# Expert passes on four column tiles, activations turned in 32x32 blocks by VectorE

## The reference

```python
g = jnp.minimum(xb @ w_gate[e] + b_gate[e], SWIGLU_LIMIT)
u = jnp.clip(xb @ w_up[e] + b_up[e], -SWIGLU_LIMIT, SWIGLU_LIMIT)
act = g * jax.nn.sigmoid(SWIGLU_ALPHA * g) * (u + 1)
return act @ w_down[e] + b_down[e]
...
ys = lax.map(expert_block, (xs, block_e)).reshape(n_blocks * EXPERT_BLOCK, D)
y_pairs = ys[dest] * pair_gate[:, None]
return jnp.zeros_like(h).at[pair_tok].add(y_pairs)
```

## Time and profile before

| | |
|---|---|
| median of 3 runs | 1791.53 us (1791.15 to 1792.47) |
| the profiled execution | 1791.65 us, of which the span of instructions 1789.8 us |
| TensorE matmul (PE) busy | 1760.1 us, 98% of the span |
| TensorE weight loads (PEld) busy | 888.5 us, 50% |
| VectorE (DVE), ScalarE (ACT) busy | 39%, 21% |
| L1504, the expansions, 2112 records | 466.1 us busy |
| L1566, the down product, the 1036 records that read the ring | 229.5 us busy |
| L1515 combine, L1472 gather, L1485 biases | 67.6, 62.2 and 37.0 us busy |
| expert weights | 2 MB a load, median 25 to 28 us from issue to landing |
| mean granted TensorE clock | 0.998 of full speed |

### The profile page before, as it was taken

How to read it: one execution, slowest core, us unless ns; L and a number is a source line. 1 busy time by engine, 2 the same in 40 slices (tenths; PEclk the granted TensorE clock), 3 DMA queues, 4 the chain that set the end, 5 groups by cost and what they waited for, 6 DMA issues and landing times. The chain is left out here.

```text
span 1789.8 us, 21732 instructions
## 1 busy us (share of the span) xinstructions
PE 1760.1 (98%) x8267; PEld 888.5 (50%) x8268; DVE 689.4 (39%) x1369; ACT 368.0 (21%) x740; POOL 62.7 (4%) x55
## 2 busy tenths in 40 slices
PE   8999999999999999999999999999999999999998
PEld 6855533333333333333333334798445579864454
DVE  1774411111111111111111112666667757747765
ACT  2222311111111111111111113333221022222201
POOL 0000000000000000000000000450000000000000
PEclk9999999999999999999999999999999999999999
DMA  9967799999999999999999999733466653126462
GB/s 376 374 256 312 314 409 428 430 431 431 431 431 432 431 432 430 432 431 431 432 431 431 432 431 399 216 141 141 143 224 193 219 188 142 48 94 235 148 203 96
DMA packets 106570, 565.10 MB, mean 316 GB/s; under 512 B 19624, under 2 KB 42893, under 8 KB 80781
## 3 DMA queue, kind: packets, MB, share of 16 engines
q1 hardware_dynamic: 105588, 562.93, 78.1%
q10 hardware_dynamic: 922, 1.36, 0.3%
HBM read 553.78 MB, written 2.10 MB: 311 GB/s over the span
## 5 line engine op out<-in xcount | busy, mean ns | idle before, releaser
L1504 PE MATMUL ps<-ring,xs 128*64 128x512 f32 x2112 | 466.1, 593 | 6.2 <-DMA ring<-in_w_up 3.7
L1504 PEld LDWEIGHTS ps<-ring,xs 128*64 128x64 f32 x2112 | 150.9, 137 | 310.3 <-issue 294.0
L1566 PE MATMUL ps<-ring,actT 128*64 128x512 f32 x1036 | 229.5, 595 | 0.0
L1640 DVE TENSOR_SCALAR hT<-ps 128x512 f32<-128x512 f32 x33 | 22.8, 691 | 445.2 <-PE ps L1504 445.2
L2548 PE MATMUL ps<-ring 128*128 128x512 f32 x448 | 193.1, 593 | 1.1 <-DVE early_consts L2935 1.1
L2548 PEld LDWEIGHTS ps<-ring 128*128 128x128 f32 x448 | 108.6, 243 | 84.9 <-issue 61.0
L1566 PEld LDWEIGHTS ps<-ring,actT 128*64 128x64 f32 x1036 | 71.6, 137 | 155.6 <-issue 129.6
L1642 DVE TENSOR_SCALAR hT<-ps 128x512 f32<-128x512 f32 x33 | 22.8, 691 | 265.0 <-PE ps L1504 265.0
L2523 PE MATMUL ps<-ring,hT 128*128 128x512 f32 x192 | 84.8, 593 | 0.0
L2905 DVE TENSOR_TENSOR ring<-ring 128x2048 f32<-128x2048 f32 x32 | 72.6, 2286 | 13.5 <-PE ps L2523 7.7
L1617 ACT COPY y<-ps 128x512 f32<-128x512 f32 x33 | 19.3, 585 | 246.5 <-PE ps L1566 246.5
(11 more groups left out here) (523 smaller groups left out, 1987.6 us busy)
## 6 DMA issues: line engine op xcount, KB each, us to landing
ring<-in_w_gate SPq DMA_DIRECT2D x64, 2048.0 KB, 26.9
ring<-in_w_up SPq DMA_DIRECT2D x64, 2048.0 KB, 25.1
ring<-in_w_down SPq DMA_DIRECT2D x62, 2048.0 KB, 27.7
ring<-in_mlp_w SPq DMA_DIRECT2D x16, 2048.0 KB, 8.6
ring<-in_mlp_w SPq DMA_DIRECT2D x32, 1024.0 KB, 5.6
ring<-in_w_mod SPq DMA_DIRECT2D x8, 2048.0 KB, 12.9
ring<-in_odd_w_in SPq DMA_DIRECT2D x6, 2048.0 KB, 10.6
ring<-in_w_mod SPq DMA_DIRECT2D x16, 512.0 KB, 10.9
```

Source lines behind the costliest of these rows:

```text
L1504: mm = pe.matmul(ps[SLOTS * half:SLOTS * (half + 1), bank, :], xs[:, c % 4, c // 4 * SLOTS:(c // 4 + 1) * SLOTS], weights(v, 8 * part + c) ...
L1566: mm = pe.matmul(ps[SLOTS * half:SLOTS * (half + 1), Y, :], actT[:, f % 4, f // 4 * SLOTS:(f // 4 + 1) * SLOTS], moving, start=(f == 0), s ...
L1640: v.tensor_scalar(g, ps[:, G, :], LIMIT, None, ALU.min).then_inc(g_ok, 1)
```

## The change

The 64 slots of a pass become two groups of 32 (`TILE`), and the array is used as four column tiles of 32 instead of two of 64. Column tile j holds, for both groups, the 128 columns from 128 j of each half of the 1024 columns: group 0 lies in columns 0 to 255 of the bank, group 1 in columns 256 to 511 (`tile_columns`, `group_columns`). So an expansion has, for each block of weight rows, eight matmuls of 256 columns in place of two of 512, and the down product four matmuls of 512 columns in place of two. The biases become eight matmuls of 512 columns, each reading its 256 bias columns twice (`twice`), and a new matmul of one column goes ahead of them.

With this layout the activations can be turned inside 32x32 blocks. VectorE does it with two block transposes straight from `g` into `actT` (`turn_tiles`), which gets the shape 128 x 8 x 64. TensorE's four transposes of the activations, ScalarE's copy of them and the semaphore between them go. TensorE no longer waits for `act_ok` and `xs_sb` there, but for `u_ok`. The gathered tokens are turned by TensorE as before, and the gather and `combine` keep their shapes. SyncE's last load of the stage waits for `selt_ps` in place of `xt_ps`.

```diff
--- before.py
+++ after.py
@@ -28,7 +28,7 @@
 IN_W = FOUR + QLAT + KVLAT + ROPE
 EPS = 1e-6
 EXPERTS, TOPK, FF = 32, 4, 1024
-SLOTS = 64
+SLOTS, TILE = 64, 32
 SPARE = (SEQ * TOPK) // (SLOTS + 1)
 PASSES = EXPERTS + SPARE + 1
 LIMIT, ALPHA = 7.0, 1.702
@@ -1366,6 +1366,27 @@
     return w[0, bass.ds(e, 1), k * 512:(k + 1) * 512, :].rearrange("e (p a) n -> p (e a) n", p=P)
 
 
+def twice(a):
+
+    return a.rearrange("p (g k) n -> p g k n", g=1).to_broadcast([a.shape[0], 2, a.shape[1], a.shape[2]])
+
+
+def tile_columns(a, j):
+
+    return a.rearrange("p (k j n) -> p k j n", k=2, j=4)[:, :, j, :]
+
+
+def group_columns(a, g):
+
+    return a[:, SEQ * g:SEQ * (g + 1)].rearrange("p (k n) -> p k n", k=2)
+
+
+def turn_tiles(v, out, src, g):
+
+    blocks = src[:, SEQ * g:SEQ * (g + 1)].rearrange("p (k r a) -> p k a r", k=2, a=4)
+    return v.transpose(out[:, :, TILE * g:TILE * (g + 1)].rearrange("p (k a) n -> p k a n", k=2), blocks)
+
+
 def stage_experts(nc, m, t):
 
 
@@ -1379,14 +1400,14 @@
     xrow = s.sb("xrow", [P, 512])
     xs = s.sb("xs", [P, 4, P])
     g, u, sig = (m.hT[:, 2 * j:2 * j + 2, :].rearrange("p c n -> p (c n)") for j in range(3))
-    actT = s.sb("actT", [P, 4, P])
+    actT = s.sb("actT", [P, C, SLOTS])
     y = s.sb("y", [P, 512])
     m.even_in = [m.lasting(f"even_in{k}") for k in range(4)]
 
 
     G, U, Y, TURN, COMB = 0, 1, 2, 3, 4
-    w_free, xt_ps, down_ps, selt_ps, comb_ps, actT_ps, bias_ps, total_ps = (
-        m.sem(f"e_{n}") for n in ("w_free", "xt_ps", "down_ps", "selt_ps", "comb_ps", "actT_ps", "bias_ps", "total_ps"))
+    w_free, xt_ps, down_ps, selt_ps, comb_ps, bias_ps, total_ps = (
+        m.sem(f"e_{n}") for n in ("w_free", "xt_ps", "down_ps", "selt_ps", "comb_ps", "bias_ps", "total_ps"))
     x_ps = m.gather_ps
     sel_ok, selg_ok, now_ok, g_ok, u_ok, act_mul, act_ok = (
         m.sem(f"e_{n}") for n in ("sel_ok", "selg_ok", "now_ok", "g_ok", "u_ok", "act_mul", "act_ok"))
@@ -1459,7 +1480,7 @@
             sp.dma_start(columns(12)[:, :, 384:512], src[:, :, KWN:KWN + P]).then_inc(m.even_in[0], 16)
             sp.dma_start(columns(16), src[:, :, NQ:NQ + 512]).then_inc(m.even_in[1], 16)
             sp.dma_start(columns(20), src[:, :, MQ:MQ + 512]).then_inc(m.even_in[2], 16)
-            sp.wait_ge(xt_ps, n + 1)
+            sp.wait_ge(selt_ps, n)
             sp.dma_start(columns(0), src[:, :, MK:MK + 512]).then_inc(m.even_in[3], 16)
 
         @block.tensor
@@ -1479,12 +1500,12 @@
                 mm.then_inc(xt_ps, 1)
 
             def biases(parts):
-                for half in range(2):
+                for j in range(4):
                     for part, bank in parts:
                         a = EXPERTS * part
-                        mm = pe.matmul(ps[SLOTS * half:SLOTS * (half + 1), bank, :], now[a:a + EXPERTS, :],
-                                       m.brows[a:a + EXPERTS, half * 512:(half + 1) * 512], start=True, stop=False,
-                                       skip_group_check=True)
+                        row = tile_columns(m.brows[a:a + EXPERTS, :], j)
+                        mm = pe.matmul(ps[TILE * j:TILE * (j + 1), bank, :], now[a:a + EXPERTS, 0:TILE],
+                                       twice(row), start=True, stop=False, skip_group_check=True)
                 mm.then_inc(bias_ps, 1)
 
             def arrived(v, turn, k):
@@ -1500,10 +1521,11 @@
                 for c in range(C):
                     if c % 4 == 0:
                         arrived(v, turn, 2 * part + c // 4)
-                    for half in range(2):
-                        mm = pe.matmul(ps[SLOTS * half:SLOTS * (half + 1), bank, :], xs[:, c % 4, c // 4 * SLOTS:(c // 4 + 1) * SLOTS],
-                                       weights(v, 8 * part + c)[:, half * 512:(half + 1) * 512], start=False, stop=(c == C - 1),
-                                       skip_group_check=True)
+                    for g in range(2):
+                        for j in range(4):
+                            mm = pe.matmul(group_columns(ps[TILE * j:TILE * (j + 1), bank, :], g), xs[:, c % 4, c // 4 * SLOTS + TILE * g:c // 4 * SLOTS + TILE * (g + 1)],
+                                           tile_columns(weights(v, 8 * part + c), j), start=False, stop=(c == C - 1),
+                                           skip_group_check=True)
                     if c % 4 == 3:
                         mm.then_inc(w_free, 1)
 
@@ -1541,13 +1563,10 @@
                 pe.wait_ge(y_sb, i + 1)
                 pe.wait_ge(selT_sb, i + 1)
                 combine(False, comb_ps)
-                pe.wait_ge(xs_sb, i + 2)
-                pe.wait_ge(act_ok, i + 1)
-                for b in range(4):
-                    mm = pe.transpose(ps[:, TURN, b * P:(b + 1) * P], g[:, b:512:4], ident)
-                mm.then_inc(actT_ps, 1)
+                pe.wait_ge(u_ok, i + 1)
                 pe.wait_ge(now_ok, i + 1)
                 pe.wait_ge(selT_sb, i + 2)
+                pe.matmul(ps[0:SLOTS, G, 0:1], now[0:EXPERTS, :], m.brows[0:EXPERTS, 0:1], start=True, stop=True, skip_group_check=True)
                 biases(((0, G), (1, U)))
                 pe.wait_ge(actT_sb, i + 1)
                 for f in range(C):
@@ -1563,9 +1582,10 @@
                             moving = later_row(m)[:, cols]
                         else:
                             moving = weights(v, 16 + f)[:, cols]
-                        mm = pe.matmul(ps[SLOTS * half:SLOTS * (half + 1), Y, :], actT[:, f % 4, f // 4 * SLOTS:(f // 4 + 1) * SLOTS],
-                                       moving, start=(f == 0), stop=(f == C - 1),
-                                       skip_group_check=True)
+                        for g in range(2):
+                            at = SLOTS * half + TILE * g
+                            mm = pe.matmul(ps[at:at + TILE, Y, :], actT[:, f, TILE * g:TILE * (g + 1)], moving, start=(f == 0),
+                                           stop=(f == C - 1), skip_group_check=True)
                     if f == C - 1:
                         mm.then_inc(down_ps, 1)
                     elif f % 4 == 3:
@@ -1611,17 +1631,15 @@
                 act.wait_ge(selt_ps, i + 1)
                 act.wait_ge(comb_ps, i + 1)
                 act.copy(selT[:].rearrange("p i n -> p (i n)"), ps[:, G, 0:QT * P]).then_inc(selT_sb, 1)
-                act.wait_ge(actT_ps, i + 1)
-                act.copy(actT[:].rearrange("p b n -> p (b n)"), ps[:, TURN, :]).then_inc(actT_sb, 1)
                 act.wait_ge(down_ps, i + 1)
                 act.copy(y[:], ps[:, Y, :]).then_inc(y_sb, 1)
-            act.activation(actT[:, 0, 0:1], m.eps[:, 0:1], ACT.Sqrt)
+            act.activation(sig[:, 0:1], m.eps[:, 0:1], ACT.Sqrt)
 
         @block.vector
         def _(v):
             n = passes(v)
             iota = cst(m, "iota", P, 0, SLOTS)
-            twice = iota.rearrange("p (a n) -> p a n", a=1).to_broadcast([P, 2, SLOTS])
+            both = iota.rearrange("p (a n) -> p a n", a=1).to_broadcast([P, 2, SLOTS])
 
             with v.Fori(0, n) as i:
                 v.wait_ge(x_ps, i + 1)
@@ -1630,13 +1648,13 @@
                 ins.then_inc(sel_ok, 1)
                 v.wait_ge(selt_ps, i)
                 for j in range(QT):
-                    ins = v.tensor_scalar(selg[:, j, :, :], twice, m.keys[:, j, bass.ds(i, 1)], m.gates[:, j, bass.ds(i, 1)],
+                    ins = v.tensor_scalar(selg[:, j, :, :], both, m.keys[:, j, bass.ds(i, 1)], m.gates[:, j, bass.ds(i, 1)],
                                           ALU.is_equal, ALU.mult)
                 ins.then_inc(selg_ok, 1)
                 v.wait_ge(bias_ps, i + 1)
                 v.tensor_copy(now[:], m.pick[:, bass.ds(i + 1, 1)].to_broadcast([2 * EXPERTS, SLOTS])).then_inc(now_ok, 1)
                 v.wait_ge(w_free, i * 5 + 2)
-                v.wait_ge(actT_ps, i)
+                v.wait_ge(actT_sb, i)
                 v.tensor_scalar(g, ps[:, G, :], LIMIT, None, ALU.min).then_inc(g_ok, 1)
                 v.wait_ge(w_free, i * 5 + 4)
                 v.tensor_scalar(u, ps[:, U, :], -LIMIT, LIMIT, ALU.max, ALU.min).then_inc(u_ok, 1)
@@ -1645,6 +1663,10 @@
                 v.wait_ge(act_mul, i + 1)
                 v.wait_ge(sig_ok, i + 1)
                 v.tensor_tensor(g, u, sig, ALU.mult).then_inc(act_ok, 1)
+                v.wait_ge(act_ok, i + 1)
+                for h in range(2):
+                    ins = turn_tiles(v, actT, g, h)
+                ins.then_inc(actT_sb, 1)
     s.stack.close()
```

## The result

| | before | after |
|---|---|---|
| median of the runs taken together | 1791.34 us | 1841.76 us (1840.82 to 1843.45) |
| ratio | | 1.0282, 95% interval 1.0264 to 1.0300 |
| the profiled execution, its span | 1791.65, 1789.8 | 1842.1, 1840.2 us |
| mean granted TensorE clock | 0.998 | 0.991 |
| instructions in the profile | 21732 | 36926 |

A forecast was written before the change was run, and what follows sets the result against it. Weight loads and TensorE were both near their limit, with 3.0 us to spare. A pass 0.56 us longer and five jumps of 3.4 us gave 13.8 us until 779 us and 13.7 after: +27.5, 1819.0 us, range 1801 to 1836.

The forecast's parts named there:

- The law: Expert stage: if TensorE's pass grows by d, the end moves by max(0, 20.6 d - 7.9) + 12.4 d.
- Transposes removed: Before the biases: TensorE's four activation transposes lay under the wait for ScalarE's selT copy; gain 0 to 0.03 us.
- Four-tile expansions: Gate and up expansions: 32 slots take 6.91 us instead of 6.87, +0.04 each, +0.08 a pass.
- Tile shapes around the gather: Gather alone stays 64 wide, so shape changes on the way in and back cost +0.28 us a pass.
- Biases and the one-column matmul: Before the down product: +0.16 us for the added matmul's shape, +0.03 for 16 bias records instead of 8.
- The pass: One TensorE pass of the expert stage: all terms sum to +0.56 us, period 27.55.
- The queue's lead between passes: TensorE's sequencer, 2.1 to 2.4 us ahead: +0.03 a pass; 0.4 us sticks out at each of five turn ends.
- Refetching the loop's code: Five jumps to the loop's head: a 14.5-page body doesn't stay stored, so each jump costs 3.4 us (1.5 to 4.6).
- Rival A: TensorE's loop code stays resident, a jump costs 0.4 us: +12.5 us, 1804; chance 0.24.
- B: Not slower: shape changes around the gather are free and the one-column matmul hides; 1793 or 1788.5; chance 0.11.
- C: Eight bias tiles don't run together: pass +1.4 us, end +55 with refetch, 1847; chance 0.05 together with D.
- D: Four 32-wide tiles don't overlap, each expansion doubles: far over 1850; chance 0.05 together with C.

The follow-up runs named there:

- b_short: The kernel before with only the first 128 tokens gathered, so TensorE's pass is 0.86 us shorter: 1790.13 us, ratio 0.9993 (0.9983 to 1.0003).
- a_sel_y: The changed kernel with the turned gate matrix in bank Y; the down product, not the biases, waits for ScalarE's copy: 1820.03 us, single run.
- a_gather32: The changed kernel with the gather, too, on four column tiles of 32: 1833.27 us in a single run, pass 27.23 us.
- b_split_one: The kernel before with the gate product's matmuls cut into two of 256 columns, loop body 6.8 pages: 1791.90 us, ratio 1.0001.
- b_split_both: The kernel before with gate and up products' matmuls both cut into two of 256 columns, loop body 8.0 pages: 1817.00 us, ratio 1.0140.
- a_tiny_loads: The changed kernel loading 32 KB in place of each 2 MB expert part, TensorE's program unchanged: 1820.54 us, single run.
- a_unrolled: The changed kernel with TensorE's loop of six turns over five experts written out: 1808.01 us, ratio 1.0091.
- b_unrolled: The kernel before with TensorE's loop of six turns over five experts written out, as a control: 1797.28 us, ratio 1.0031.
- a_all2: The changed kernel with loop written out, gather on four tiles and turned gate matrix in bank Y: 1806.53 us, ratio 1.0075.

## Why the prediction was right in direction and wrong in size

- **The resource that sets the end.** Right. The law (early passes hide 7.9 us, late ones nothing) gives 50.0 for the measured terms, and 50.4 was measured. b_short bears out the cap on the other side.
- **Transposes removed: nothing gained.** Right. The idle time of 0.62 us before the one-column matmul, ended by ScalarE's selT, stands where they stood, and a_sel_y takes it out.
- **VectorE's transposes.** 1.15 us for the pair, forecast 1.1 to 1.3; done 1.2 us before the down product. Never on the path.
- **Four-tile expansions.** +0.08 forecast. 128 records take 7.09 and 7.11 us busy for 7.04, +0.12 together. Right to 0.04.
- **Tile shapes around the gather.** +0.28 forecast, 0.28 measured by a_gather32.
- **Biases and the one-column matmul.** +0.19 forecast. From the one-column matmul to the down product 1.19 us pass, where it was 1.02 from the biases on: +0.17. Eight tiles do run at once.
- **The pass.** +0.56 forecast, +0.52 measured, 27.51 us.
- **The queue's lead between passes.** Forecast +0.03; nothing shows in the undisturbed passes. At a turn's end 0.4 us was to stick out, five times. Nothing did: each pass before a jump is 5.7 to 6.1 us longer than 27.51, which is what its branch takes beyond 0.22. The sequencer was 2.5 us ahead there, as much as it needs: it was through with the pass at 395.1 us, and the next would have begun at 397.67 (6.89 us after the down product, as in the steady pass).
- **Refetching the loop's code.** The mechanism, its five places and the missing waits for weights were forecast, and b_split_one and b_split_both show it by itself. Its size was wrong, and here the whole error lies: 3.4 us a jump forecast, 8.1 measured, (8.1 - 3.4) x 5 = 24 us. Two terms failed. The wait for the page was put at 3.0 us, between the 1.1 us of a packet and the 4.2 us of a small transfer; it took 6.0 us on average (branches of 6.0 to 6.3 less 0.22), of which 3.6 to 4.0 went by before the page began to move. 3.0 is nearly what a_tiny_loads shows for an idle queue (3.3), and the row of 4.2 us was taken from a stretch with a lighter load, 1286 to 1378 us, with the DMA engines 40 to 60% busy. I took it for an upper bound, which made the bound of a jump 4.6 us, and it was none. The second term was missing altogether: behind each pause 1.4 to 2.9 us were lost to a stretch at half clock, 11 us in the five. I had not looked for it in the trace of before, as nothing in this stage pauses for more than 1.0 us there. The first stage would have been a place to look: in its first 50 us TensorE is idle for 7.0 us and the mean granted clock is 0.97, the only such stretch before the expert passes.
- **Rival A**, the loop staying resident, was priced at 1804. The kernel that comes nearest, a_unrolled, takes 1808; its pages slow the weights, a cost that no sum of the prediction had. The rivals B, C and D did not happen.

## What to carry to other kernels

Count instructions as well as time when a matmul is cut into narrower tiles: a loop's body that stops fitting into the engine's store turns each jump to its head into a pause, and written-out code is traffic beside the weights. Before an engine is relieved of work, look at which wait the work was covering; here four transposes covered a copy by ScalarE, and taking them away uncovered it. And take the price of a fetch from a stretch of the trace in which the queues are as full as at the place where it will happen.

## What the runs showed of the hardware that was not expected

- A jump of TensorE out of its stored code takes 3.3 to 3.8 us with nearly idle DMA queues (a_tiny_loads) and 5.8 to 6.6 us behind the full weight queue: 1.0 to 1.4 or 3.5 to 4.2 us until the page starts, 0.9 us for the page, 1.4 to 1.5 us after it. Inside the store the jump takes 0.22 us.
- The store held a loop body of 6.8 pages and not one of 8.0.
- A page of 16 KB of code delays a full weight queue by 0.2 us on average, in steps of 1.2 to 1.7 us at one load in some seven pages (b_unrolled, a_unrolled, a_all2).
- After each of 27 pauses of 3.7 to 6.2 us, in six kernels, TensorE ran partly at 1.2 GHz, in a stretch that cost 1.4 to 2.9 us; after pauses of 2.9 to 3.3 us (a_tiny_loads) only in two cases of five, at a cost of 1.7 us.
- Eight tiles of 32x32 with 512 columns each run side by side: 16 records in 1.09 us busy, as 8 records on four tiles before.
